# Mixture-of-experts visits of two sizes: one loop that alternates them, instead of one loop after the other

## The reference

```python
for e in range(N_EXPERTS):
    act = jax.nn.silu(hf @ w_gate[e]) * (hf @ w_up[e])
    out = out + combine[:, e:e + 1] * (act @ w_down[e])
```

## Time and profile before

| | |
|---|---|
| median of three runs | 3374.93 us |
| the profiled execution, its own time | 3381.49 us |
| its span from first to last instruction | 3379.8 us |
| TensorE busy | 2632.9 us, 78% of the span |
| VectorE / ScalarE / GpSimd busy | 871.4 / 415.0 / 279.9 us |
| moved by DMA | 744.57 MB, mean 220 GB/s |
| weight matrices of experts loaded | 63 + 63 + 63 of the later two mixtures, 16 + 16 + 16 of the first |
| hidden products of single / double visits | 49 of 421 ns / 30 of 688 ns |

### The profile page before, as it was taken

The page is one execution under the profiler, slowest core; times in us unless marked ns, Lnnn a source line. Parts: engine busy times, 40 slices in busy tenths (PEclk is TensorE's granted clock), DMA queues, the critical chain, the costliest instruction groups (busy, mean ns, idle before and its releaser), DMA issues. The chain is left out here.

```text
span 3379.8 us, 34102 instructions
## 1 busy us (share of the span) xinstructions
PE 2632.9 (78%) x11124; PEld 1356.0 (40%) x11124; DVE 871.4 (26%) x1534; ACT 415.0 (12%) x779; POOL 279.9 (8%) x415
## 2 busy tenths in 40 slices
PE   6996779768985998867775999649699837777692
PEld 4431144234433553524432444225376424433240
DVE  1221253000004795410000000160357520000004
ACT  1011140000001001000000000010055100000000
POOL 3001140200001000020000000000000010000001
PEclk8998878898997998879997999869899959999796
DMA  9426611779954112279997899442001149999783
GB/s 345 135 78 222 210 13 57 292 315 343 335 218 142 50 50 77 75 279 421 423 423 305 323 333 338 166 137 75 0 13 36 33 177 418 423 423 422 273 296 118
DMA packets 150429, 744.57 MB, mean 220 GB/s; under 512 B 13552, under 2 KB 15264, under 8 KB 101168
## 3 DMA queue, kind: packets, MB, share of 16 engines
q1 hardware_dynamic: 100784, 592.46, 45.3%
q0 software_dynamic: 35568, 115.04, 9.9%
q10 hardware_dynamic: 13968, 35.66, 2.8%
HBM read 664.24 MB, written 79.46 MB: 220 GB/s over the span
## 5 line engine op out<-in xcount | busy, mean ns | idle before, releaser
L681 PE MATMUL ps<-w_ring,arena 128*64 128x256 f32 x3136 | 369.1, 390 | 133.3 <-DMA w_ring<-in_e_up 59.7
L604 PE MATMUL ps<-w_ring,arena 128*128 128x512 f32 x960 | 429.4, 602 | 7.2 <-ACT arena L600 7.2
L232 PE MATMUL ps<-x_feat,w_ring 128*128 128x512 f32 (+1 forms) x1152 | 421.5, 528 | 7.9 <-ACTq L145 3.7
L681 PEld LDWEIGHTS ps<-w_ring,arena 128*64 128x64 f32 x3136 | 221.5, 140 | 285.2 <-DMA w_ring<-in_e_gate 91.8
L232 PEld LDWEIGHTS ps<-x_feat,w_ring 128*128 128x128 f32 x1152 | 220.6, 192 | 208.0 <-issue 192.9
L604 PEld LDWEIGHTS ps<-w_ring,arena 128*128 128x128 f32 x960 | 183.3, 194 | 227.0 <-issue 222.5
L706 PE MATMUL ps<-w_ring,arena 128*64 128x512 f32 x784 | 182.3, 607 | 41.0 <-DMA w_ring<-in_e_down 35.4
L626 PE MATMUL ps<-w_ring,arena 128*128 128x512 f32 x480 | 211.3, 593 | 2.3 <-ACT arena L621 2.3
L324 PE MATMUL ps<-w_ring,x_feat 128*128 128x512 f32 x448 | 198.4, 606 | 13.7 <-ACTq L145 12.1
L955 PE MATMUL ps<-w_ring,fcol 128*2 128x512 f32 x384 | 182.0, 630 | 3.2 <-issue 2.3
L690 DVE TENSOR_TENSOR arena<-arena,ps 128x256 f32<-128x256 f32 x49 | 20.7, 421 | 629.9 <-PE ps L681 629.9
(11 more groups left out here) (272 smaller groups left out, 2326.9 us busy)
## 6 DMA issues: line engine op xcount, KB each, us to landing
w_ring<-in_e_gate SPq DMA_DIRECT2D x63, 2048.0 KB, 17.5
w_ring<-in_e_up SPq DMA_DIRECT2D x63, 2048.0 KB, 17.9
w_ring<-in_e_down SPq DMA_DIRECT2D x63, 2048.0 KB, 17.2
w_ring<-in_ada_w SPq DMA_DIRECT2D x24, 2048.0 KB, 10.2
w_ring<-in_w_gate SPq DMA_DIRECT2D x16, 2048.0 KB, 10.7
w_ring<-in_w_up SPq DMA_DIRECT2D x16, 2048.0 KB, 10.4
w_ring<-in_w_down SPq DMA_DIRECT2D x16, 2048.0 KB, 8.6
arena<-expert_rows ACTq DMA_DIRECT2D x39, 512.0 KB, 8.6
```

Source lines behind the costliest of these rows:

```text
L232: mm = nc.tensor.matmul(pair(j)[:, t0:t1], w[:, k, c0:c0 + P], x_feat[:, k, t0:t1], start=k == 0, stop=k == KT - 1)
L604: mm = nc.tensor.matmul(bank(2 + part), blk_feat[:, s, k, :], chunk_view(slot, FF)[:, k, :], start=k == 0, stop=k == KT - 1)
L681: mm = nc.tensor.matmul(bank(2 + part)[self.H * c:self.H * (c + 1), 0:256], blk_feat[:, s, i, self.H * h:self.H * (h + 1)], w[:, h, i, 256 ...
```

## The change

Both kinds run in one loop. A round now holds a single visit and then a double visit; the loop has as many rounds as the larger of the two kinds (16, 32 and 32). The barriers `singles1`, `singles2`, `singles3` are gone. Each kind has three weight slots of its own: the doubles slots 0, 1, 2 of `w_ring`; the singles slot 3 of `w_ring`, the first 4096 columns of `x_feat` (not in use during the experts) and the first 4096 of the arena. In the first visit gate uses slot 0 and up slot 1; from then on gate uses slot 2, up slot 0, down slot 1. Each kind has its own counters `free` and `landed0` to `landed2`; `w_free` and `w_landed` no longer count experts. The single visits get their own small buffers and PSUM bank 7 for their output; banks 0 to 4 are shared by both kinds, so TensorE waits in addition for the other kind's silu, hidden product and feature copy. The layer-norm rows for the combine go to other places (`last_rows`). Before the scatter is over, SyncE now starts four matrices (gate and up of both kinds) where it started two.

```diff
-        self.chunks = 3 * (self.doubles + self.singles) + 4
+        self.turns = max(self.doubles, self.singles) // 4
992.89 7.13 PE L626 class Singles
-            def slot(self, slot, part):
-                return w_ring[:, slot, :].rearrange("p (h n) -> p h n", h=2)
+            def slot(self, slot):
+                return (w_ring[:, RING - 1, :], feat_slot, rows_slot)[slot]
992.89 7.13 PE L626 moe_sp (new)
+            for kind in kinds:
+                for slot, (part, w) in enumerate((("gate", gate), ("up", up))):
+                    matrix = source(kind, w, 0, part)
+                    if kind.follows(slot, chunks.n) >= 0:
+                        sp.wait_ge(w_free, kind.follows(slot, chunks.n) + 1)
+                    load(kind, slot, matrix)
...
+            sp.wait_ge(*count(f"{name}.scattered", 32 * m.T))
+            with sp.Fori(0, m.turns) as turn:
+                for b in range(4):
+                    i = turn * 4 + (b + 1)
+                    for n, kind in enumerate(kinds):
...
+                        with sp.If(i < n_used[n]):
+                            matrix = source(kind, gate, i, "gate")
+                            freed(1)
+                            load(kind, 2, matrix)
+                            matrix = source(kind, up, i, "up")
+                            freed(2)
+                            load(kind, 0, matrix)
...
+                        with sp.If(i < n_used[n] + 1):
+                            matrix = source(kind, down, i - 1, "down")
+                            freed(3)
+                            load(kind, 1, matrix)
992.89 7.13 PE L626 moe_blocks_pe (new; n is 0 for singles, 1 for doubles)
+            turn_rows(0, 0, 16)
+            pe.wait_ge(*count(at(0, "feat"), 1))
+            turn_rows(1, 0, 16)
+            for part in range(2):
+                gate_or_up(0, 0, part, part, 1)
...
+            with pe.Fori(0, m.turns) as turn:
+                for b in range(4):
+                    s = (b + 1) % 2
+                    i = turn * 4 + (b + 1)
+                    for n in range(2):
+                        other = 1 - n
+                        with pe.If(i < n_used[n]):
+                            pe.wait_ge(*count(at(n, "feat"), i + 1))
+                            pe.wait_ge(*count(at(other, "silu"), i + n))
+                            gate_or_up(n, s, 0, 2, i)
+                            turn_hidden(n, 1 - s, i)
+                            pe.wait_ge(*count(at(other, "hid"), i + n))
+                            gate_or_up(n, s, 1, 0, i + 1)
+                            pe.wait_ge(*count(at(other, "feat"), i + 1 + n))
+                            turn_rows(n, 1 - s, turn * 32 + 16 * ((b + 2) // 2 + 1))
+                            down(n, 1 - s, i)
                         with pe.Else():
+                            pe.drain().then_inc(summed[at(n, "free")], 2)
+                            pe.sem_inc(summed[at(n, "turned")], 1)
...
992.89 7.13 PE L626 stages (on each of the four compute engines, three times)
-            moe_blocks_pe(pe, "moe1", Singles(MOE1), chunks)
-            stage(pe, "pe", "singles1")
-            moe_blocks_pe(pe, "moe1", Doubles(MOE1), chunks)
+            moe_blocks_pe(pe, "moe1", MOE1)
             stage(pe, "pe", "experts1")
```

More of the change, by code:

```diff
@@ L398, in moe_sems @@
                 shared(name, route_counts(m))
-                for kind, n in (("single", m.singles), ("double", m.doubles)):
-                    shared(f"{name}.{kind}", visit_counts(n))
+                for kind in ("double", "single"):
+                    for part, total in visit_counts(4 * m.turns).items():
+                        shared(name, {f"{kind}.{part}": total})
                     new_sems(f"{name}.{kind}", "stored")
@@ L736, in moe_sp, with source @@
-            if kind.kind == "single":
-                sp.wait_ge(*count(f"{name}.scattered", 32 * scatter_tiles[name]))
-            with sp.Fori(0, kind.n // 4) as turn:
+            sp.wait_ge(*count(f"{name}.table", 1))
+            kinds = (Singles(m), Doubles(m))
+            n_used = [kind.used(sp) for kind in kinds]
+            def source(kind, w, visit, part):
+                e = sp.value_load(expert_of[0:1, bass.ds(visit + kind.table_at, 1)], min_val=0, max_val=m.E - 1)
+                return kind.weights(w, e, part)
@@ L739, in moe_sp @@
+            for kind in kinds:
+                if kind.follows(2, chunks.n) >= 0:
+                    sp.wait_ge(w_free, kind.follows(2, chunks.n) + 1)
+            sp.wait_ge(*count(f"{name}.scattered", 32 * m.T))
+            with sp.Fori(0, m.turns) as turn:
                 for b in range(4):
                     i = turn * 4 + (b + 1)
[L741 to L756, removed]
@@ new lines, in moe_blocks_act, with moe_blocks_dve, at, hidden @@
+            for n in range(2):
+                for s in range(2):
+                    act.wait_ge(*count(at(n, f"rows{s}"), 16 * (2 * m.turns + 2)))
+        def moe_blocks_dve(dve, name, m):
+            kinds = (Singles(m), Doubles(m))
+            def at(n, part):
+                return f"{name}.{kinds[n].kind}.{part}"
+            def hidden(n, s, i):
+                dve.wait_ge(*count(at(n, "silu"), i + 1))
+                kinds[n].hidden(s).then_inc(summed[at(n, "hid")], 1)
+            def outputs(n, s, i, done):
+                dve.wait_ge(summed[at(n, "free")], done)
+                dve.wait_ge(*count(at(n, "out_free"), i))
+                kinds[n].take_outputs(s).then_inc(summed[at(n, "y_copied")], 1)
+            n_used = [kind.used(dve) for kind in kinds]
+            for n in range(2):
+                dve.sem_inc(summed[at(n, "y_copied")], 1)
+                dve.wait_ge(*count(at(n, "free"), 3))
+                hidden(n, 0, 0)
+            with dve.Fori(0, m.turns) as turn:
@@ L1590, in _ @@
             stage(act, "act", "route1")
[L1591 to L1593 removed]
+            moe_blocks_act(act, "moe1", MOE1)
             stage(act, "act", "experts1")
@@ L1970, in load_rows, with load_last_rows @@
                     load(rows[:, i, :], row.partition_broadcast(P))
+            def load_last_rows(*given):
+                for i, row in enumerate(given):
+                    load(last_rows[i], row.partition_broadcast(P))
             def mod(layer, cond, part):
```

387 lines of the change are left out of this document (182 added, 205 removed).

## The result

The changed kernel takes 3458.4 us (median of four runs, 3450.55 to 3460.95), the one before 3374.95: ratio 1.0241, 95% interval 1.0222 to 1.0259. It is slower by 2.4%; 3.9% faster was forecast, and the time lies outside the range.

What follows compares the result with a forecast made beforehand. Singles were taken as bound by DMA, doubles by TensorE, one stage after the other. Visits -188.9 us, start +26 and tail +31.6 gave -131.3, hence a median of 3244 us, range 3200 to 3325.

Steps and rivals of the forecast that it cites:

- What bounds the kernel: Expert visits: singles wait for weights from DMA, doubles for TensorE, two stages with opposite limits, one after the other.
- A paired round, 34.0 us: A single plus a double visit: 33.7 us of TensorE and 0.3 us of added waits, where the pair took 38.08.
- The choice of 33.5 over 36.0: DMA time per paired round: 33.5 us with the double's transfers at 422 GB/s, rather than 36.0 at 370 GB/s.
- B: Paired rounds: loads of both kinds delay each other, rounds stay at 38 us; 3350 us, half-way 3296; together chance 0.15.
- The handover: Between singles and doubles in each mixture: the lost time, 37.6 us in the second mixture, would be saved.
- Start, +26: Ahead of the visits: four early matrices cost 4, 8 and 8 us, first double rows 2 us per mixture; 26 lost.
- The length of the loop: TensorE's combined loop of about 1500 to 1600 instructions just fits its store; straight-line fetching costs nothing.
- Tail: After the last down product: 54 instead of 26 empty rounds, 28 more at 1.13 us, 31.6 us lost.
- Left-over rounds: Rounds where one kind is over: left singles 16.13 us each as before, left doubles 21.95 + 1.13 us.
- edges and lead: Visits: 9.5 us of edges per mixture; 8 us credited in the second and third for matrices loaded ahead.
- Rival A: Tail: the loop leaves TensorE's store, 27 empty pairs fetch 1.6 lines at 2 us; 86 us, 3330 us; chance 0.11.
- Rival C: TensorE's loop: straight-line fetching in the rounds stalls too; 3498 us at 1.5 us per crossing; chance 0.06.

Runs made afterwards that it cites:

- e4: The changed kernel, with gate and up of the first double visit asked for after the scatter instead of before it: 3445.45 us.
- e1: The changed kernel, with TensorE's loop alone cut from four to two rounds per turn and twice as many turns: 3274.08 us.
- e9: The changed kernel with two TensorE rounds per turn, plus 28 never-executed products in four blocks behind branches in the loop: 3691.07 us.
- e2: The kernel before the change, with TensorE's two loops lengthened from four to eight rounds per turn: 3434.55 us.
- e6: The changed kernel with two TensorE rounds per turn, plus 28 never-executed products in one block behind a branch: 3294.48 us.

## Why the prediction was wrong

- **What bounds the kernel**: right. Two stages of opposite limits; together they fill both resources (98.99 of 100 us, share 1.01).
- **A paired round, 34.0 us**: right, 34.07, and by its parts too: 98.99% of that is 33.7 us of TensorE and 0.3 us of idle time, as summed. The choice of 33.5 over 36.0 for the DMA engines held; B is out.
- **The handover**: gone, as said. TensorE's longest idle time inside the visits is 9.3 us, where it was 25 to 28.
- **Start, +26**: of the right size, +20.0, of which e4 gives 15.2 to the early loads ahead of mixtures two and three. My 8 there was 7.6; the first mixture lost 1.5 instead of 6, which is less than that stretch varies from kernel to kernel.
- **The step that failed is "The length of the loop"**, and with it two terms of the sum. From the rows of a loop that I put at 840 instructions I concluded that one of 1500 to 1600 is kept, though the earlier trace rows shows nothing for a loop of that length. The first has 925 to 937, since I left out waits, branches and semaphore operations; the second has 1667 to 1699 and is fetched every turn. So two terms that I had priced as if nothing were fetched came out too small, and e1 shows by how much.
  - *Tail*: 28 more empty rounds at 1.13 us made 31.6; measured 148.9. Fetching is 110.6 of the 117 too little. The other 7 stand in e1's tails as well (75.6 against 37.3 before, +38.3): there an empty pair costs 3.0 us, not 2.26, though 27 pairs of that difference would be 20 us.
  - *Left-over rounds*: left singles stood at 16.13 us and took 18.2 in the third mixture, left doubles at 23.08 and took 23.7 to 33. Fetching is 70.3 us of the 97 that the visits fell short; 13 of these 70 are at the jump back of the paired rounds. The other 27 are in e1's visits too. Its left doubles take 23.65 us and its paired rounds 34.07, which makes 4 together; its left singles, 16.0, give 3 back; and what is left for edges and lead is 15.9, 12.7 and 10.0 us where I had 9.5, 1.5 and 1.5, so 26. They fit with edges of 10 to 16 and no credit for the lead; that split wasn't tested.
- **Rival A** named the mechanism, but as a matter of the tail alone at 2 us per line, 86 us, and I gave it 0.11. Its fetches were 43 at 2 us; the tails have 60 packets, 3.1 us apart, and the left rounds, where every visit of one kind jumps over the other's code, pay as well.
- **Rival C** gave 3498, the nearest time, for a reason that the runs refute for this kernel: lines fetched in a straight stretch cost nothing in rounds of 34.07 us. The time was lost where TensorE jumps: back to the loop's head, and over the code of empty rounds.
- By the Trainium skill (Runtime: NRT & Kernel Launch, Instruction fetch mechanics), TensorE's store takes 2048 instructions. That a loop shorter than this is kept doesn't follow: here 1667 were fetched every turn. As a size the figure isn't refuted, since the second mixture of e9 kept some 1750. The two lines that the same section gives to the store, if they are meant for TensorE too, would have a loop of 58 KB fetched each turn, and the earlier trace rows and the 93 KB of e2 disagree. Its rule that a taken branch out of what is stored stalls for a fetch is what the tail shows, with 28 packets in 86 us. I had used the figure to drop the rule.

What would have shown it ahead: the length of the loop was known, its neighbours in the profile were half as long, and 27 empty pairs jump over all of it. Both ends of such an unknown belonged in the range.

## What to carry to other kernels

Count all instructions of a TensorE loop's body, waits and branches too, and compare with the longest body that the profile shows running without instruction packets. If it is longer, shorten the turn before anything else, above all where branches skip most of it. Pass a hardware loop's unused turns with one branch per turn. Two stages, one bound by DMA and one by TensorE, are worth alternating: 3345 to 3225 us here, once both were done.

## What the runs showed of the hardware

- TensorE ran loops of 58 KB (before) and 93 KB (e2) without fetching them again and fetched those of 104 to 106 KB (after) and 115 to 117 KB (e2) each turn. No limit between them follows: loops of 109 KB with dead code were kept in e6 and in one mixture of e9. What is replaced by what is open.
- A fetch on its own, in a chain of jumps, takes 3.1 us per packet of 16.4 KB; in a straight stretch of paired rounds it was hidden (seven packets in 100 us, TensorE busy 98.99).
- Instructions that never run cost 20 us as one block (40 turns, with their compare and branch) and 417 us as four, where the jumps touch them. The same loop suffers at one place of the program (third mixture's visits 715.0 us, against 486.4 in e1) and hardly at another (second, 601.8 against 585.7). Which placement does harm was not measured.
